# An encoder trunk on one core: the opening transposes x as it lands, and its scale is applied behind the first products

## The reference, cut to what matters

```
h = rms_norm(x, mix_norm_g[0])     # y = x * rsqrt(mean(x*x) + 1e-6), then y * g
gb, gc, hc, q, k, v, g = split_cols(h @ ev_w_in, (512,) * 7)
u    = gc * hc                                  # short convolution over the sequence
a    = gb * (w0 * u[t-1] + w1 * u[t] + w2 * u[t+1])
q, k = rotary(q), rotary(k) / 8                 # angles: positions * inv_freq
o    = group_rms_norm(bidirectional_retention(q, k, v))
x    = x + concat([a, silu(g) * o]) @ ev_w_out
```

## Time and profile before

| | us |
|---|---|
| median of 3 runs | 1638.57 |
| lowest, highest | 1638.51, 1638.99 |
| the profiled execution | 1639.78 |
| its span, first to last instruction | 1637.9 |
| TensorE busy | 1614.5 (99%) |
| VectorE busy | 1270.1 (78%) |
| ScalarE busy | 1036.1 (63%) |
| GpSimd busy | 59.7 (4%) |

### The profile page before, as it was taken

How to read it: one execution, slowest core, us unless ns; L and a number is a source line. 1 busy time by engine, 2 the same in 40 slices (tenths; PEclk the granted TensorE clock), 3 DMA queues, 4 the chain that set the end, 5 groups by cost and what they waited for, 6 DMA issues and landing times.

```text
span 1637.9 us, 22669 instructions
## 1 busy us (share of the span) xinstructions
PE 1614.5 (99%) x8508; PEld 1378.4 (84%) x8508; DVE 1270.1 (78%) x1070; ACT 1036.1 (63%) x908; POOL 59.7 (4%) x54
## 2 busy tenths in 40 slices
PE   7999999999999999999999999999999999999997
PEld 6998989998887798888888888888888888888886
DVE  7776646454567765798888888888888888888897
ACT  5443445544356544677777777777777777777775
POOL 1000000000000101100000000000000000000100
PEclk9999999999999999999999999999999999999999
DMA  9644445555554354899999999999989999999994
GB/s 351 206 160 151 159 128 174 186 180 189 172 182 153 129 202 173 293 357 381 374 390 373 382 382 377 382 380 368 383 292 359 382 392 363 381 393 358 396 394 168
DMA packets 226030, 474.70 MB, mean 290 GB/s; under 512 B 7698, under 2 KB 52964, under 8 KB 225972
## 3 DMA queue, kind: packets, MB, share of 16 engines
q1 hardware_dynamic: 221552, 459.01, 77.8%
q0 software_dynamic: 3104, 10.66, 1.9%
q10 hardware_dynamic: 1316, 4.24, 0.6%
HBM read 466.01 MB, written 7.87 MB: 289 GB/s over the span
## 4 chain that ended last, share of the span: by engine, by line
PE 91%; DVE 4%; ACT 2%; DMA 1%; issue 1%; POOL 0%; POOLq 0%; ACTq 0%; SPq 0%; DVEq 0%
PE ps L2328 35%; PE ps L2351 18%; PE ps L1860 15%; PE ps L1826 9%; PE ps L1846 4%; PE ps L2089 4%; DVE w_lo L394 2%; PE ps L2336 1%; ACT w_hi L390 1%; PE ps L2001 1%; PE ps L2021 1%; DMA raw<-in_moe_w_gate 1%; PE ps L2115 0%; PE ps L1955 0%; PE ps L2316 0%
## 5 line engine op out<-in xcount | busy, mean ns | idle before, releaser
L394 DVE TENSOR_TENSOR w_lo<-raw,w_hi 128x2048 fp32r<-128x2048 f32 x430 | 980.3, 2291 | 224.1 <-ACT w_hi L390 222.6
L390 ACT ACTIVATE w_hi<-raw 128x2048 fp32r<-128x2048 f32 x430 | 823.7, 1918 | 297.4 <-PE ps L2328 107.6
L2328 PE MATMUL ps<-w_hi,e_hi 128*128 128x512 f32 x896 | 355.3, 397 | 0.7 <-DVE w_lo L394 0.5
L2328 PE MATMUL ps<-w_hi,e_lo 128*128 128x512 f32 x896 | 349.7, 390 | 0.0
L2328 PE MATMUL ps<-w_lo,e_hi 128*128 128x512 f32 x896 | 349.0, 390 | 0.0
L2328 PEld LDWEIGHTS ps<-w_hi,e_hi 128*128 128x128 f32 x896 | 168.2, 188 | 37.9 <-DVE w_lo L394 2.6
L2328 PEld LDWEIGHTS ps<-w_hi,e_lo 128*128 128x128 f32 x896 | 168.2, 188 | 36.0
L2328 PEld LDWEIGHTS ps<-w_lo,e_hi 128*128 128x128 f32 x896 | 168.5, 188 | 33.4
L2351 PE MATMUL ps<-w_hi,at_hi 128*128 128x512 f32 x448 | 176.1, 393 | 0.4 <-DVE w_lo L394 0.3
L2351 PE MATMUL ps<-w_hi,at_lo 128*128 128x512 f32 x448 | 174.6, 390 | 0.0
L2351 PE MATMUL ps<-w_lo,at_hi 128*128 128x512 f32 x448 | 174.3, 389 | 0.0
(11 more groups left out here) (362 smaller groups left out, 1720.3 us busy)
## 6 DMA issues: line engine op xcount, KB each, us to landing
raw<-in_moe_w_up SPq DMA_DIRECT2D x112, 1024.0 KB, 7.8
raw<-in_moe_w_gate SPq DMA_DIRECT2D x110, 1024.0 KB, 7.5
raw<-in_moe_w_down SPq DMA_DIRECT2D x110, 1024.0 KB, 7.3
raw<-in_xa_wkv SPq DMA_DIRECT2D x16, 1024.0 KB, 5.2
raw<-in_ev_w_in SPq DMA_DIRECT2D x14, 1024.0 KB, 9.5
raw<-in_od_w_in SPq DMA_DIRECT2D x12, 1024.0 KB, 5.1
raw<-in_ffd_w_gate SPq DMA_DIRECT2D x11, 1024.0 KB, 5.4
raw<-in_ffd_w_up SPq DMA_DIRECT2D x11, 1024.0 KB, 5.3
```

Source lines behind the costliest of these rows:

```text
L390: nc.scalar.activation(w_hi[:, n % CUT, :], at_, ACT.Copy).then_inc(hi_cut, 1)
L394: nc.vector.tensor_tensor(w_lo[:, n % CUT, :], place(n, r, behind)[0], w_hi[:, n % CUT, :].bitcast(F32), ALU.subtract).then_inc(lo_cut, 1)
L2328: mm = T.matmul(ps[:, bank, :], s, m, start=(h == 0 and k == 0 and j == 0), stop=(h == 1 and k == 3 and j == 2))
```

## The change

x is transposed as it is, in two halves, without its factor r. The gain of the columns is still applied where the transposed tiles are cut. r goes in later: into the rotary tables for q and k, as a column factor into v and g, as r*r into gc and once more as r into gb*conv(...) for the convolution, where it is needed along the free axis; for that TensorE multiplies ones by a diagonal of r (L2000) and GpSimd squares the row (L588) and multiplies the convolution's result by it (L591).

- SyncE issues the constants first, then the left half of x, slab 0 in two pieces, the right half of x, slab 1 in two pieces, slab 2, the ten transfers of gains, slab 3, the memory, slabs 4 and 5. ScalarE issues only the positions (now one per partition, in two transfers) and the eight rows of the first gain.
- TensorE multiplies ones by ones 13 times, turns the first gain, does four idle transposes instead of 16, turns the left half of x, works two of the four k tiles of slab 0, and turns the right half.
- VectorE computes the angles behind the rest of slab 2; then the columns, x's root, the rest of slab 3, the tables times r, the diagonal, and the rotation of q.

Its core as a diff (what is left out are the same moves on ScalarE and the declarations):

```
@@ block.sync
-            sp.dma_start(X[:, :, :], x[0].rearrange("(t p) n -> p t n", p=P)).then_inc(in_x, 16)
             sp.dma_start(const[:, :], consts[:, 0:3 * P + 56]).then_inc(in_const, 16)
+            x_half(0, in_x)
+            for i in range(2):
+                s = slabs["evq"][i]
+                for half_, arrived in ((0, first_in[i]), (1, raw_in[i])):
+                    sp.dma_start(shaped(raw[:, i, 1024 * half_:1024 * half_ + 1024], 2),
+                                 s[:, 2 * half_:2 * half_ + 2, :]).then_inc(arrived, 16)
+                if i == 0:
+                    x_half(1, in_x2)
...
@@ block.gpsimd
+            nc.gpsimd.memset(one_row, 1.0).then_inc(pool_link, 1)
...
+                if name == "ret":
+                    pool.wait_ge(acc_free, BANKS["evc"] + 6)
+                    nc.gpsimd.tensor_tensor(ev_u, ev_u, r_row.unsqueeze(1).broadcast_to([P, 4, 256]),
+                                            ALU.mult).then_inc(conv_r, 1)
...
@@ block.scalar
-            act.wait_ge(acc_free, BANKS["evc"] + 6)
+            act.wait_ge(conv_r, 1)
             nc.scalar.activation(a_hi[:, 0:4, :], ev_u, ACT.Copy).then_inc(conv_hi, 1)
...
@@ block.vector
+            dve.wait_ge(n_sq, 2)
+            means("x0", 2, D)
+            V.tensor_copy(rkeep[:, :], rstd[:, 0:2]).then_inc(n_out, 2)
+            dve.wait_ge(n_out, 2)
+            cut_lo(dve, 3)
...
@@ block.tensor
+            pe.wait_ge(pool_link, 2)
+            for _ in range(13):
+                T.matmul(ps[:, 3, 0:P], one_row, one_row, start=True, stop=True)
             pe.wait_ge(in_const, 16)
...
+            turn_raw(0)
...
             gemm_t("evk", 1, a_hi, a_lo)
+            pe.wait_ge(setup_v, 4)
+            T.matmul(ps[:, 4, 0:256], one_row, r_diag, start=True, stop=True).then_inc(setup_t, 1)
             gemm_t("evv", 1, a_hi, a_lo)
```

More of the change, by code:

```diff
@@ L181, in trunk_kernel @@
         table = sb("table", [1, 24], I32)
+        sb("table_end", [P, 16])
         with ExitStack() as s:
@@ L413, in _ @@
                     load(sp, n + i, s)
-                if name == "evq":
-                    sp.wait_ge(in_row, 160)
+                    if name == "evk" and i == 0:
+                        for row, v in (("mem", mem_norm_g), ("x0", mix_norm_g[0]), ("x1", mix_norm_g[1]),
+                                       ("xa0", xa_norm_g[0]), ("xa1", xa_norm_g[1]), ("ffn", ffn_norm_g[0]),
+                                       ("moe", ffn_norm_g[1]), ("ret", ev_ret_gn_g[0]), ("dif", od_gn_g[0])):
+                            r, k = ROWS[row], v.shape[0] // P
+                            sp.dma_start(rows[r:r + k, :], v.rearrange("(k p) -> k p", p=P)).then_inc(in_row, 16)
+                        sp.dma_start(rows[ROWS["conv"]:N_ROWS, :],
+                                     ev_conv_w[0].rearrange("j (k p) -> (j k) p", p=P)).then_inc(in_row, 16)
+                if name == "evk":
                     sp.dma_start(tbt, mem[0].rearrange("(t p) n -> p t n", p=P)).then_inc(in_mem, 16)
@@ L593, in link @@
                 act.wait_ge(act_link, links[0])
[L596 to L603, removed]
+            for t in range(2):
+                act.dma_start(pos_i[:, t:t + 1],
+                              positions[0, t * P:(t + 1) * P].rearrange("(p o) -> p o", o=1)).then_inc(in_pos, 16)
+            act.dma_start(rows0[:, :], mix_norm_g[0].rearrange("(k p) -> k p", p=P)).then_inc(in_row0, 16)
             def squares(name, src, into=rot[:, :, :].rearrange("p a n -> p (a n)")):
@@ L1054, in freed @@
                 ins.then_inc(acc_free, w)
[L1056 to L1080, removed]
             c1 = 6.28125
@@ L1086, in _, with first_rest @@
             big = 12582912.0
+            dve.wait_ge(setup_t, 1)
+            r0 = ROWS["x0"]
+            V.tensor_copy(cols[:, r0:r0 + KT], ps[:, 2, 0:KT]).then_inc(setup_v, 1)
+            def first_rest(i, c0, c1, whole, count, done):
+                dve.wait_ge(whole, count)
+                V.tensor_tensor(w_lo[:, i, c0:c1], raw[:, i, c0:c1], w_hi[:, i, c0:c1].bitcast(F32),
+                                ALU.subtract).then_inc(done, 1)
+            turn_lo("x0", a_hi, a_lo, tiles=range(2))
+            first_rest(0, 0, 512, first_hi, 1, first_lo)
+            turn_lo("x0", a_hi, a_lo, tiles=range(2, 4))
+            first_rest(0, 512, 1024, first_hi, 2, first_lo)
+            first_rest(0, 1024, 2048, hi_cut, 1, lo_cut)
+            first_rest(1, 0, 1024, first_hi, 3, first_lo)
+            turn_lo("x0", a_hi, a_lo, tiles=range(4, 8))
+            first_rest(1, 1024, 2048, hi_cut, 2, lo_cut)
+            cut_lo(dve, 2)
+            dve.wait_ge(in_pos, 32)
+            link(V.tensor_copy(pos[:, :], pos_i[:, :]))
+            dve.wait_ge(in_const, 16)
+            for t in range(2):
+                link(V.tensor_scalar(ang[:, t, :], freq, pos[:, t:t + 1], None, ALU.mult))
             link(V.tensor_scalar(turnsb[:, :, :], ang[:, :, :], 1.0 / (2 * math.pi), None, ALU.mult))
@@ L1099, in _ @@
             link(V.tensor_scalar(cos[:, :, :], cos[:, :, :], -2.0, 1.0, ALU.mult, ALU.add))
+            for t in range(2):
+                for v in (cos, sin):
+                    link(V.tensor_scalar(v[:, t, 0:32], v[:, t, 0:32], rkeep[:, t:t + 1], None, ALU.mult))
+            for t in range(2):
+                V.tensor_scalar(r_diag[:, t * P:(t + 1) * P], ident, rkeep[:, t:t + 1], None,
+                                ALU.mult).then_inc(setup_v, 1)
             def rotate(src, dst, heads, half_, f0, done):
```

107 lines of the change are left out of this document (76 added, 31 removed).

## The result

| | before | after |
|---|---|---|
| median, us | 1638.78 | 1661.49 |
| lowest, highest | 1638.51, 1639.42 | 1660.76, 1662.36 |
| runs | 4 | 4 |
| profiled execution, its span | 1639.78, 1637.9 | 1662.08, 1660.2 |

The ratio is 1.0137, with a 95% interval of 1.0124 to 1.0150. The forecast was 1637.7, its range 1634.6 to 1639.7, and slower had 5 chances in 100. Both were wrong.

The account below looks back on a forecast made before the run. TensorE was taken to bound the kernel (91% of the chain). Terms: -4.1 (slab 2) + 0.45 (diagonal product) + 2.1 (slab 4) + 0.7 (convolution) = -0.9, giving 1637.7 us, range 1634.6 to 1639.7.

Parts of the forecast that it names:

- What bounds the kernel: Whole kernel: TensorE is 91% of the chain that ended last, so time gained at the start stays unless taken back.
- At nothing: Scaled copies, gc products, positions' pieces, smaller transfers, x's squares and gain transfers cost nothing; 0 to 1 us if cover goes.
- The ones, the first product, slabs 0 and 1: Opening: ones end at 6.8, first product at 10.45, slab 2 at 22.4 without its 1.7 wait; 4.1 us gained.
- VectorE ahead of slab 4: VectorE's queue finishes slab 4's rest at 35.9, so TensorE stalls 2.1 us (bounds 1.2 to 2.6).
- The convolution: GpSimd's multiplication, 2.5 us plus 0.15 hand-over against 1.95 to spare, stalls TensorE 0.7 us (bounds 0 to 2.8).
- The sum: All terms together: -0.9 us, taking the median from 1638.57 to 1637.7.
- (a): Opening: TensorE's pace rises early, ones end at 5.75, all moves by 1.1 to 1636.6; chance early 0.14, late 0.05.
- (b): Slab 4: the stall does not come, sum -2.95, 1635.6 us; chance 0.14.
- (c): Convolution: GpSimd's multiplication takes 6.7 us, a stall of 4.9, sum +3.3, 1641.9 us; chance 0.07.
- (d): Opening: x's left half or first gains land after 8; each microsecond past 7 costs one, 1638.7 at 8; chance 0.05.

Follow-up runs that it names:

- a_base_128: Kernel after with 128 bytes of padding, so that the region begins at byte 167552, remainder 128 by 256 as before the change; 1639.43 us, ratio 1.0002.
- v_angles: `a_base_before` with VectorE's list reordered: angles moved earlier, rest of slab 3 and x's mean ahead of columns and cosines; 1636.17 us, ratio 0.9986.
- a_base_before: Kernel after with 384 bytes of padding, so that the region begins at byte 167808 again, as in the kernel before; 1638.93 us, ratio 0.9999.
- p_all_shifted: Kernel before with slabs, a tiles and region all moved to remainder 0 by 256; 1638.77 us, ratio 0.9997.
- a_base_64: Kernel after with the region 64 bytes further, at remainder 64 by 256 while the slabs stay at 128; 1644.58 us, ratio 1.0035.
- b_base_after: Kernel before, its work unchanged, with the region moved to byte 167424 as in the kernel after; 1661.38 us, ratio 1.0134.
- p_w_shifted: Kernel before with slabs and a tiles moved to remainder 0 by 256, the region left at 128 (byte 167552); 1660.71 us, ratio 1.0130.

## Why the prediction was wrong, point by point

- **What bounds the kernel**: right as far as it went (94% of the chain), but it held a step that failed: "a microsecond that TensorE gains at the start is still there at the end, unless something takes it back on the way". TensorE's pace behind the opening was taken as given.
- **"At nothing"**, the step that failed: the declarations of tiles were not among the edits that were priced. They moved the region by 384 bytes, and the runs put +22.5 us in that place, +1.4%, 25 times the forecast effect. What was at stake could be read from the trace: the experts alone have 4032 products of 512 columns, so each nanosecond on one of them is 4 us.
- **The ones, the first product, slabs 0 and 1**: right in mechanism: 6.84 for 6.8, 10.53 for 10.45, slab 2 at 22.53 for 22.4, the wait of 1.7 gone. That the marks fit to a tenth is partly luck: in the six other profiles of this opening the pace rose sooner, and the first product started up to 0.7 earlier.
- **VectorE ahead of slab 4**: right in mechanism and size (1.9 for 2.1; 36.00 for 35.9), but short of two things. The queue was summed on VectorE alone, while the squares behind slab 3's transfer hold it too: VectorE idled 0.3 for them in after and 1.0 in `a_base_128`, whose slab 4 starts 0.5 later. The other is what a wait can do to the clock: 1.85 more here. The prediction spoke of the clock only at the start. The wait of 1.7 before slab 2 in the kernel before had been followed by 1.00 throughout, and so gave no warning. All four runs of after have a mean clock of 0.997, where the runs of before have 0.998 or 0.999.
- **The convolution**: right, 0.5 for 0.7, GpSimd 2.38 for 2.5.
- **The sum**: -0.9 forecast; the same work measured -0.25 with an interval of -1.6 to +1.3, in which the forecast lies. With -0.9 and the fall's 1.85 after should have been 0.95 slower at the convolution, where it is 0.63 slower.
- **The rivals**: (a) early came, in full or in part, in six of the seven profiles of this opening; in the fullest case 0.5 of its 1.1 was taken by the gains' landing; (b) did not come until `v_angles` made it; (c) fell at 2.38; (d) fell. The slower case that came was none of them: every rival looked where the change works, and none where it only moves memory.

## What to carry to other kernels

Price the declarations as well as the instructions: list each large tile's start before and after a change, and if a tile that feeds TensorE has moved relative to the other operand, try the change with a pad that puts it back before judging it. When a profile is slower by the same share in a stage that the diff doesn't touch, compare the mean ns of equal matmuls first. And a wait of about 2 us on TensorE can cost twice its length, when the clock falls behind it.

## What the runs showed of the hardware

- Take the stationary tile (the weights that TensorE holds, here e, at or f) and the moving tile (here the slab) of a product of 512 columns, both of the rounded float32 type fp32r. Where their starts leave different remainders by 256 bytes, most products were slower, at the two differences that were run. TensorE's groups by placement (the slabs against e):

| difference, bytes | e groups, ns (hi*hi, w_hi*e_lo, w_lo*e_hi) | runs |
|---|---|---|
| 0 | 396 or 397, 390, 390 | before, `a_base_before`, `p_all_shifted` |
| 64 | 399, 392, 390 | `a_base_64` |
| 128 | 400, 394 or 395, 394 or 395 | after, `b_base_after`, `p_w_shifted` |

The means are over records of which some may be missing; the medians of the runs carry the verdict. With every other engine at rest the loss is the same, and the weight loads take 188 ns in before and after. Products of 256 columns with m, where the slab is the stationary tile, take 286 and 283 ns at 0, 284 and 283 at 128, and 281 to 277 at 64; those with a never had a difference. The tiles od and m moved too: their nine groups of 32 products with 512 columns take 1 to 6 ns more in after. Why the groups differ stays open, and so does the mechanism itself: no run tells what in the reading of the two tiles is slow.
- The granted clock fell to 0.50 behind a wait of 1.9 us (after) and one of 2.1 us (`a_base_before`), for 3 to 4 us, each time about a microsecond after TensorE had taken up work again. It stayed at 1.00 behind five other waits of 2.1 us and behind those of 2.3 (`a_base_128`) and 2.2 (`a_base_64`) at slab 4. TensorE worked 1.6 to 1.9 us longer each time.
- At the start of the program the clock's column reads 1.00 while 128x128 records come every 0.217 us instead of 0.109. How long that lasts changes from execution to execution: the 26 records of ones took 4.58 to 5.82 us in seven profiles.
